# Second block: head norms, residual rows and masks reordered; x by token rows, first weight tile in half depths, first conv unit in column halves

## What is computed

```python
def rms_norm(x, g):
    return x * rsqrt(mean(x * x, axis=-1, keepdims=True) + 1e-6) * g
for l in range(2):                       # second block
    h  = rms_norm(x, g_mix[l]) * (1 + sc1) + sh1       # and hc from ctx, 256 context tokens
    qa, ka, va, fb, qc, kc, vc = split(h @ w_in[l])    # the same for hc
    qa, ka = rms_norm(qa, q_norm), rms_norm(ka, k_norm)   # per head of 64; not qc, kc
    qa, ka, qc, kc = rope(...)                         # for x, not for ctx
    o = concat(global_attention(qa, ka, va, and ctx), fourier_mix(fb),
               window_attention(qc, kc, vc, and ctx, sink[l]))   # |i - j| <= 128
    x = x + gt1 * (o @ w_out[l])
    x = x + gt2 * swiglu(...)
    # layer 0 does the same for ctx (dense attention, without a window); layer 1 leaves ctx as it is
return rms_norm(x, g_final)
```

## Time and profile before

| | |
|---|---|
| median of 3 runs | 2317.36 us (2317.27 to 2323.43) |
| the profiled execution | 2318.68 us, span 2317.0 us |
| mean granted clock of TensorE | 0.986 |
| PE busy | 2229.0 us, 96% of the span |
| DVE busy | 1186.2 us, 51% |
| ACT busy | 448.6 us, 19% |
| chain that ended last | PE 77%, DMA 10%, DVE 8% |

### The profile page before, as it was taken

How to read it: one execution, slowest core, us unless ns; L and a number is a source line. 1 busy time by engine, 2 the same in 40 slices (tenths; PEclk the granted TensorE clock), 3 DMA queues, 4 the chain that set the end, 5 groups by cost and what they waited for, 6 DMA issues and landing times.

```text
span 2317.0 us, 24671 instructions
## 1 busy us (share of the span) xinstructions
PE 2229.0 (96%) x9725; PEld 1399.2 (60%) x9725; DVE 1186.2 (51%) x1983; ACT 448.6 (19%) x1013; POOL 3.5 (0%) x23
## 2 busy tenths in 40 slices
PE   8999999999989999999999998899999999998998
PEld 7755445544357754445444785678888887554453
DVE  3755874211157267752111357765556433687666
ACT  1001402211111014022111225320000102352010
POOL 0000000000000000000000000000000000000000
PEclk9999999999999999999999999999999999999999
DMA  8345844799953459346999520002212124403340
GB/s 337 146 175 224 363 172 173 306 423 428 428 229 146 151 201 412 118 168 272 423 428 427 231 92 18 1 1 102 81 73 87 59 92 172 155 10 145 136 172 18
DMA packets 35983, 451.41 MB, mean 195 GB/s; under 512 B 5160, under 2 KB 7066, under 8 KB 8474
## 3 DMA queue, kind: packets, MB, share of 16 engines
q1 hardware_dynamic: 32992, 447.63, 47.7%
q10 hardware_dynamic: 2874, 2.17, 0.3%
HBM read 448.73 MB, written 1.05 MB: 194 GB/s over the span
## 4 chain that ended last, share of the span: by engine, by line
PE 77%; DMA 10%; DVE 8%; DVEq 2%; issue 1%; ACT 1%; SPq 0%; ACTq 0%
PE banks L556 74%; DMA ring<-in_w_exp_up 9%; PE banks L1548 1%; DVE tiny L3027 1%; DVEq L2091 1%; PE banks L707 1%; DVE tiny L2370 1%; DMA ring<-in_w_in 1%; DVE arena L2384 1%; DVE arena L2090 1%; DVE arena L3044 0%; DVE arena L2079 0%; DVE ring L2116 0%; DVE banks L2367 0%; DVE ring L2825 0%
## 5 line engine op out<-in xcount | busy, mean ns | idle before, releaser
L556 PE MATMUL banks<-ring,arena 128*64 128x512 f32 (+2 forms) x3290 | 966.2, 554 | 18.6 <-DMA ring<-in_w_exp_up 5.8
L556 PEld LDWEIGHTS banks<-ring,arena 128*128 128x128 f32 (+1 forms) x3290 | 446.8, 167 | 506.7 <-issue 473.6
L556 PE MATMUL banks<-arena 128*128 128x128 f32 (+6 forms) x1568 | 239.7, 346 | 13.6 <-ACT arena L2044 6.9
L556 PE MATMUL banks<-X,ring 128*128 128x256 f32 x1024 | 224.1, 381 | 1.8 <-DMA ring<-in_w_in 1.2
L556 PEld LDWEIGHTS banks<-X,ring 128*128 128x128 f32 x1024 | 195.8, 192 | 30.9 <-issue 3.3
L556 PEld LDWEIGHTS banks<-arena 128*128 128x128 f32 (+2 forms) x1568 | 154.5, 176 | 72.3 <-issue 31.5
L556 PE MATMUL banks<-arena,ring 128*128 128x256 f32 (+1 forms) x736 | 178.0, 399 | 2.4 <-ACT arena L1873 2.3
L556 PEld LDWEIGHTS banks<-arena,ring 128*128 128x128 f32 x736 | 139.6, 190 | 36.3 <-issue 17.3
L2215 DVE TENSOR_TENSOR arena<-arena,banks 128x512 f32<-128x512 f32 x16 | 11.0, 687 | 258.2 <-ACT arena L1696 258.2
L556 PE MATMUL banks<-ring 128*128 128x256 f32 x616 | 137.0, 380 | 0.0
L2116 DVE TENSOR_TENSOR ring<-ring 128x2048 f32<-128x2048 f32 (+1 forms) x56 | 119.7, 2138 | 18.0 <-ACT arena L1658 12.5
(11 more groups left out here) (351 smaller groups left out, 1925.5 us busy)
## 6 DMA issues: line engine op xcount, KB each, us to landing
ring<-in_w_in SPq DMA_DIRECT2D x38, 2048.0 KB, 12.2
ring<-in_w_exp_gate SPq DMA_DIRECT2D x32, 2048.0 KB, 13.5
ring<-in_w_exp_up SPq DMA_DIRECT2D x32, 2048.0 KB, 16.6
ring<-in_w_exp_down SPq DMA_DIRECT2D x32, 2048.0 KB, 11.8
ring<-in_w_ada SPq DMA_DIRECT2D x24, 2048.0 KB, 10.9
ring<-in_w_ffn SPq DMA_DIRECT2D x22, 2048.0 KB, 7.6
ring<-in_w_out SPq DMA_DIRECT2D x8, 2048.0 KB, 13.1
ring<-in_w_down SPq DMA_DIRECT2D x8, 1408.0 KB, 6.9
```

The source lines that it names most:

```text
L556: ins = nc.tensor.matmul(out, weights, moving, start=start, stop=stop)
```

## The change

Six edits go together.

1. **Start.** x is loaded in two transfers of 128 token rows, each with its own semaphore; PE turns each as it arrives. Tile 0 is loaded in two transfers, depth chunks 0 to 3 and 4 to 7. PE makes all four output chunks over the first half of the depth, into four open banks (0, 1, 4, 5), then over the second half. ACT copies these four. ACT issues the positions behind the first twelve parameter loads.
2. **Conv unit of layer 0** of the first block: each product in two halves of 256 columns.
3. **Head norms**, both layers of the second block. Each of the four squares is multiplied with a 128 x 32 matrix (`head_pick`) that yields a head's mean in one row, into rows 32 i to 32 i + 31 of one bank. DVE adds epsilon, ACT takes the root and DVE the reciprocal once, over all rows (`head_areas`: all 512 columns in layer 0; in layer 1 256 columns of all rows and 256 more of the last 32). After n = 6 PE spreads each 32 rows over the heads' 128 with `head_spread`, contracting over 32 rows, into banks 4 to 7, and DVE multiplies from there. The two matrices come in one more row of the constant table (128 KB more). mean_h and its three memsets go.
4. **Residual rows.** XR is made by DVE from the normalised rows of the last layer norm, times the gain and plus the bias of it, which ACT loads as rows for all partitions (1 MB in all) into ring slot 5. The transposes and ACT's copies go.
5. **Masks.** In layer 0 PE adds the mask to the scores, as a product of the identity with it into the same bank; in layer 1 DVE adds it as before.
6. **Sink.** ACT takes the sink's exponential with the negated maximum as its bias, one head at a time; DVE's addition (L3032) goes.

```diff
-            sp.dma_start(raw["x"], a["x"].rearrange("(c p) d -> p c d", p=P)).then_inc(s_x, 16)
+            for tc in range(TC):
+                sp.dma_start(raw["x"][:, tc, :], a["x"][tc * P:tc * P + P, :]).then_inc(s_x[tc], 16)
...
+                    if l == 0 and i == 0:
+                        sp.dma_start(ring[:, 0, 0:TILE // 2], src[:, 0:TILE // 2]).then_inc(s_half_tile, 16)
+                        sp.dma_start(ring[:, 0, TILE // 2:TILE], src[:, TILE // 2:TILE]).then_inc(s_loaded[0], 16)
...
-                    for k in range(kh):
-                        ins = mm(bank[b][:], rows[:, k, :], w[:, k, :], start=(k == 0), stop=(k == kh - 1))
+                    for c in range(0, 512, width):
+                        for k in range(kh):
+                            ins = mm(bank[b][:, c:c + width], rows[:, k, :], w[:, k, c:c + width],
+                                     start=(k == 0), stop=(k == kh - 1), more=(c + width < 512))
...
-            pe.wait_ge(s_x, 16)
-            pe.wait_ge(*turned_input("x", "dve"))
-            tile_features(X, T, "act")
+            for tc in range(TC):
+                pe.wait_ge(s_x[tc], 16)
+                for half in range(2):
+                    transposes([raw["x"][:, tc, (4 * half + c) * P:(4 * half + c) * P + P] for c in range(4)],
+                               ring_bank("dve"), "dve")
+            x_copied = (last[2], last[3])
+            pe.wait_ge(s_half_tile, 16)
+            for half in range(2):
+                pe.wait_ge(*x_copied[half])
+                if half:
+                    next_tile()
+                for c, b in enumerate(FIRST_BANKS):
+                    for k in range(4 * half, 4 * half + 4):
+                        ins = mm(bank[b][:, 0:T], slot(0, DC, 512)[:, k, c * P:c * P + P], X[:, k, 0:T],
+                                 start=(k == 0), stop=(k == DC - 1))
...
                         if n == 4:
+                            free(4)
                             for i in range(4):
+                                pe.wait_ge(s_square, C.next("square"))
                                 m = proj_tokens(l, i)
-                                norm_sums([squares_h[:, i, 0:m]], m, mean_h, 4 + i % 2, s_square)
+                                ins = mm(bank[4][32 * i:32 * i + 32, 0:m], head_pick, squares_h[:, i, 0:m],
+                                         start=True, stop=True, more=(i < 3))
+                            full(ins, 4, "dve")
+                        if n == 6:
+                            pe.wait_ge(s_head_inv, l + 1)
+                            for i in range(4):
+                                m, r = proj_tokens(l, i), slice(32 * i, 32 * i + 32)
+                                free(4 + i)
+                                full(mm(bank[4 + i][:, 0:m], head_spread[r, :], head_roots[r, 0:m],
+                                        start=True, stop=True), 4 + i, "dve")
...
-                if l == 0:
-                    for i, b in enumerate((2, 3, 6, 7)):
-                        transposes([X[:, 4 * (i % 2) + j, (i // 2) * P:(i // 2) * P + P] for j in range(4)], b, "act")
...
+                        if masked:
+                            m, c0 = ((causal, P), (behind, 0))[qb]
+                            for par in range(2):
+                                ins = mm(banks[:, SCORE_BANKS[s % 2] + par, c0:c0 + P], ident[:], m[:],
+                                         start=False, stop=True)
...
+            dve.wait_ge(s_ln_rows, 32)
+            dve.wait_ge(s_rows_a, 2 * DEPTH * TC)
+            for tc in range(TC):
+                tt(rows_gained[:, tc, :], acc[:, tc, :], ln_gain, ALU.mult)
             for l in range(DEPTH):
                 nt = tokens2(l)
                 if l == 0:
                     rms(T, 4, 0, 8, 4)
+                    drain()
+                    for tc in range(TC):
+                        tt(XR[:, tc, :, 0:T], row_parts(rows_gained[:, tc, :]), row_parts(ln_bias), ALU.add)
```

98 lines of the change are left out of this document (64 added, 34 removed).

## The result

The changed kernel takes 2293.1 us in the median of four runs (2289.0 to 2295.4), the kernel before 2317.6 in the runs beside it. The ratio is 0.9888, with a 95% interval of 0.9871 to 0.9904. The medians differ by 24.5 us. The profiled execution took 2292.4, its span is 2290.6 (before: 2318.7 and 2317.0): 26 us gained between the two traces, where the forecast's sum, made against that trace, was 19.6.

A forecast was written before the change was run, and what follows sets the result against it. TensorE's waits were taken to bound the kernel: for x, before layer 0's third attention unit, and for VectorE in the attention units. Gains 2.7 + 9.3 + 0.6 (clock) + 4.8 + 2.2 = 19.6 us gave 2298, range 2292 to 2306.

The forecast's parts named there:

- First conv unit in column halves: First block, layer 0: 28 records of 512 columns become 56 of 256; gain zero, bounds -0.3 and +0.3 us.
- Start: Loads of x and tile 0: first product at 11.2 instead of 13.86, gain 2.7 us, bounds 0.5 and 3.5.
- Rival (c): At the start, the half tile lands with other bytes under way; gain 0.5, time 2300 us, chance 0.05.
- Nothing behind the start takes the 2.7 back: After the start: later tiles move up with PE, even in the transfer-bound expert stage, so 2.7 us stays gained.
- Head norms: Second block, layer 0: third attention unit starts 9.3 us earlier, bounds 6.2 and 9.4; sums and spreads 0.95 each.
- Rival (a): Head norms' row and column groups do not run side by side; spreads 3.5 us, time 2303.8, chance 0.11.
- Residual rows: Second block: DVE's extra multiplies and additions are covered by its idle 40 us; gain zero.
- rival (d): The 1 MB of gain and bias rows delays the second block's weights some 2.5 us; time 2300.3, chance 0.03.
- Masks and sinks: Second block, layer 0: windowed rounds of 11.6 us instead of 13.88; gain 4.8, bounds 2 and 7.
- Rival (b): Layer 0's windowed rounds hardly shrink, 12.8 us each; gain 2 instead of 4.8, time 2300.6, chance 0.09.
- Layer 1: Second block: 0.8 us from sums and spreads, 1.4 from 0.24 less per windowed unit; together 2.2, bounds 0 and 3.
- Rival (e): TensorE stays at the lower clock through layer 0's windowed units; slower, time 2327.5 us, chance 0.02.

The follow-up runs named there:

- e1: The changed kernel with the first conv unit's products back in whole 512-column pieces; 2301.4 us, ratio 0.9927.
- e2: The kernel before with only the first conv unit's products in two column halves; 2311.6 us, ratio 0.9968.
- e4: The kernel before with the changed start and the conv unit's column halves, second block as before; 2305.8 us, ratio 0.9941.
- e3: The kernel before with only the start changed; 2313.8 us, ratio 0.9975.
- e13: The kernel before with 128 waits that are met at once (64 instructions) in front of TensorE's first wait; 2310.5 us, ratio 0.9962.
- e6: The changed kernel with positions and frequencies issued ahead of ScalarE's twelve small loads again; 2294.9 us, ratio 0.9900.
- e17: The changed kernel itself, run again on the same chip as two late follow-ups; 2290.4 us, ratio 0.9869.
- e7: The kernel before with changed start, conv unit halves and head norms; residual rows, masks and sinks as before; 2293.8 us, ratio 0.9889.

## Why the prediction was right or wrong

The time is inside the range, but that is no credit to the sum: 7.6 us of the 26 come from an effect that no term of the sum and no rival has.

- **What bounds the kernel: wrong by omission.** I took waits that had a releaser. The 5.1 us on "issue" were in the same view and longer than the 1.7 in the attention units. This is where most of the error lies: 7.6 us.
- **First conv unit in column halves, zero: the step that failed.** As arithmetic it was right: 256-column records at half the time. But the edit adds 56 instructions to PE's code ahead of a jump, and that was worth 7 to 8 us, against bounds of -0.3 and +0.3 (e1, e2, e4 against e3; e13 with the place alone). I priced an edit by what its instructions do and not by what they push along.
- **Start: mechanism right, size wrong.** The first product came 5.0 earlier, against 2.7 and a bound of 3.5. "11.2" is what the old order of ScalarE's queue gives (10.89 in e6). The step that failed is "ScalarE's queue now issues positions behind twelve small loads; their user ... is wanted long after": I priced the moved transfer by its own user only, and not by x and tile 0, which no longer queue behind it. 2.0 us. Another 0.6 is mean_h's memsets, which GpSimd no longer has ahead of PE's first transpose. The slow clock, 1.5, "left as it is", was 1.4 less in the changed kernel's trace; as a slow beginning comes and goes with either start (28.14 in e13, 28.58 in e17), that part may be luck. Rival (c) is refuted.
- **"Nothing behind the start takes the 2.7 back": not so in these two traces.** 2.0 went between 384 and 640, most of it by the clock and not by the change. In the stretch 384 to 420, before and after, the granted clock is 0.91 and 0.86:

```profile
384.00:420.00 36.00, 33.79 (x184) 22.75 (x184) 20.91 (x59) 13.36 (x26) 0.00 (x0) 0.91 0.30 118
```

```profile
384.00:420.00 36.00, 34.14 (x187) 22.55 (x185) 18.47 (x53) 11.86 (x22) 0.00 (x0) 0.86 0.42 163
```

  That is 36 x 2 x 0.09 = 6.5 us at 1.2 GHz in place of 2.4 against 10.1; 3.6 more at half speed are 1.8 of work. Of waits for the experts' weights (in_w_exp_up) there are 6.5 us, before 5.8. How the 2.0 divide between the two is not shown.
- **Head norms: right.** 9.1 of 9.3, with the spreads at 1.14. Rival (a), 3.5 for them, is refuted. Sums and spreads are each 0.1 to 0.2 over the 0.95 that packing alone would give. Of the 0.6 for the clock 0.3 came (12.85 from third unit to the next mark before, 12.51 after).
- **Residual rows: zero, as far as seen.** PE's x transposes are gone and nothing waits for the gain and bias rows; rival (d) did not happen. They had no run of their own; e7 without them is 0.3 longer from the head sums to the third unit.
- **Masks and sinks: near in size, wrong in cause.** 3.9 for 5.4 with the clock's part. "I take the middle, 11.6" was 12.11. The term was set against 13.88 as if that were all VectorE's steps, but 1.3 of it is the slow clock (12.59 at the full one). Of the 1.77 gained in a full round 1.3 are clock, which either edit brings by a shorter wait, and 0.5 are the sinks' step; the mask addition is not what the round waits for. The 0.6 for the clock was counted for the first round only. Rival (b), 12.8, was nearer for the masks alone (12.58).
- **Layer 1: right in kind, 1.4 for 2.2.** Units 3.34 apart instead of 3.58, 0.24 each, as forecast, in five of the six intervals: 1.1 of 1.4. Of the 0.8 for sums and spreads 0.3 came. The other 1.3, ahead of layer 1's sums, lie in no edit: the granted clock is 0.91 instead of 0.83 from 1540 to 1560 of the kernel before and 0.97 instead of 0.93 from 1935 to 1985, with the same two long waits there (2.65 and 3.94).
- **Rival (e), slower clock in the rounds: refuted.** Granted clock 1.00 in all three.
- **Open:** 1.3 us lost behind layer 1's attention, of which 0.35 is one longer wait for VectorE (5.06 for 4.71).

## What to carry to other kernels

Read the longest wait on "issue" like any other: if a piece of instructions is fetched inside it, look for a jump ahead of it in the compiled program, and try a few dozen instructions more or less before anything else. Price a moved transfer by everything queued behind it, not by its own user. Where two edits relieve the same chain, run each alone: here the smaller one carried the gain and the larger one added nothing to it. And set stretches against each other at the same granted clock: a round of 13.88 at 0.88 was one of 12.59 at the full clock, and the masks' whole gain was that they kept a wait short enough for the clock to stay up.

## What the runs showed of the hardware

- A jump of TensorE over 367 instructions costs 5.1 to 5.7 us (five traces), 2.3 (one) or nothing (all others), by where its ends lie against the fetched pieces, plus 1.8 to 2.4 us of slow clock in the 16 records behind it (8.8 to 9.4 for 7.03).
- Waits of PE for VectorE in the windowed rounds of layer 0, over 19 traces: at 19 of 29 waits of 1.7 or 1.8 us the granted clock fell to 1.2 GHz, at none of 28 waits of 0.9 to 1.5. One fall costs a round 1.3 us (13.87 for 12.59 in e4).
- 400 waits that are met at once, 200 instructions, held PE until 23.6 us; 128 of them were hidden under the wait for x (first transpose at 8.79, as without).
- Time from the router (384.37 in the kernel before) to the end of the experts, without the jump's wait, grows with the time at 1.2 GHz just behind the router: 260.1 to 260.8 with 3.4 us of it (six traces), 260.6 to 262.4 with 6.8 (eight), 262.9 and 263.2 with 10.2, 263.7 to 264.2 with 13.7 (three). It differs between executions of the same kernel (262.9 and 264.1 for the changed one), so up to 4 us between two single traces can be this alone.
